# FFN gate/up: chunks 5 and 6 by seven block products

## The chip, the cores and the metric

The kernel runs on one core of a Trainium2 chip. The metric is the device time of one execution in microseconds; the time before is the median of three runs.

## The reference

Three transformer blocks on 256 rows of 1024 features, in float32. Five times in all an FFN is computed, and around them other mixers and embeddings, which the change doesn't touch:

```python
def rms_norm(x, g):
    x32 = x.astype(jnp.float32)
    y = x32 * lax.rsqrt(jnp.mean(x32 * x32, axis=-1, keepdims=True) + EPS)
    return (y * g.astype(jnp.float32)).astype(x.dtype)

def swiglu(h, w_gate, w_up, w_down):
    return (jax.nn.silu(h @ w_gate) * (h @ w_up)) @ w_down
...
        x = x + 0.5 * swiglu(rms_norm(x, g[0]), ffn_w_gate[i, 0], ffn_w_up[i, 0], ffn_w_down[i, 0])
```

The gate and up matrices are 1024x2816, the down matrix 2816x1024.

## The kernel before, in words

**Work.** The 256 rows are two tiles of 128 (tt), the 1024 features eight tiles of 128 (k). The 2816 hidden columns are eleven chunks of 256 (numbered 0 to 10). For a chunk, gate and up columns stand side by side, so that one matmul of 128x512 makes both. The rows are kept transposed and split into a high part (`hth`, rounded to the matmul's type) and a low part (`htl`, the rest); so are weights (`wh`, `wl`). A product of two such numbers is three matmuls (`product`, L273): high by low, high by high, low by high.

**Chunk.** A chunk's gate/up takes 8 k x 2 tiles x 3 = 48 matmuls in two half chunks of 24, called a (k 0 to 3) and b (k 4 to 7) here. They land in PSUM banks 0 and 1 (2 and 3 for chunk 1). The rms scale `rstd` of a row is applied after them. ScalarE does the silu of the gate half (L794), VectorE multiplies it by the up half (L869). The product must be transposed for the down matmuls: VectorE turns 32x32 blocks (L876), ScalarE's queue sends them to DRAM (`move_out`, L799) and back in another order (`move_in`, L803); this way there and back is called the bounce below. Then ScalarE makes the high part (L809), VectorE the low part (L882), and TensorE does the down of that chunk, 24 matmuls into banks 4 to 7, which hold the FFN's result. In the loop the down of chunk c-1 follows the gate/up of chunk c. Chunk 0 and the last are turned by TensorE itself (L666).

**Ring of weights.** Every half chunk and every down has a slot of 128x2048 floats (1 MB). An FFN has 33 slots, in the order a0 b0 a1 b1 d0 a2 b2 d1 a3 b3 d2 and so on. `raw`, `wh` and `wl` have room for three slots each. SP's queue loads a slot when the split of the slot three before it is done (`split_ready`); ScalarE makes its high part when it has landed and TensorE is through with the slot three before (`weights_used`); VectorE makes its low part, the split (L894, outside of the loop L247), and TensorE waits for that.

**Order.** There is no scheduler. Each engine's program is written out by hand: `ffn_load` for SP's queue, `ffn_pe`, `ffn_act`, `ffn_dve`. Within one engine everything goes in that order, and an engine that waits holds up what stands behind. In chunk c of the loop VectorE does: split of d(c-1), low part of product c-1, split of a(c+1), multiply of c, block transpose of c, split of b(c+1). ScalarE does: move_in of c-1, high part of slot d(c-1), of product c-1, of slot a(c+1), silu of c, high part of slot b(c+1), move_out of c. The loops are hardware loops (`Fori`) over chunks 2 to 9.

## Time and profile before

| | |
|---|---|
| median of 3 runs | 1306.96 us (1306.62 to 1307.1) |
| the profiled execution | 1307.18 us, its span 1305.4 us |
| TensorE matmul busy | 1289.2 us, 99% of the span |
| VectorE busy | 846.8 us, 65% |
| ScalarE busy | 654.5 us, 50% |
| GpSimd busy | 83.1 us, 6% |
| HBM read | 243.38 MB |
| mean granted TensorE clock | 0.998 |

The span reaches from the first to the last instruction; the time of an execution is a little longer. Busy times are the union of an engine's instructions. Matmuls overlap in the pipeline, so a busy TensorE need not be one at its peak; the distance from start to start tells what one costs. The page cuts the span into 40 slices: TensorE is busy 90% or more in each but the last, and the DMA engines are 60 to 70% busy in most slices of an FFN.

### The profile page before, as it was taken

What the parts mean: (1) busy time and instruction counts of PE and PEld (TensorE: products, weight loads), DVE (VectorE), ACT (ScalarE), POOL (GpSimd) and SP (SyncE); (2) the same over time, 40 slices, a digit from 0 to 9 for tenths busy, and PEclk for the clock granted to TensorE, in tenths of its full rate; (3) what the DMA queues carried; (4) which work ended last, traced back from release to release, by engine and by line L of the source; (5) the groups of instructions that cost most, each with busy time, mean ns of one, the idle gap of its engine ahead of it and who ended that gap; (6) DMA issues with size and microseconds to landing.
All of it is one profiled execution on the core that took longest, in us unless ns stands there. A gap on an engine that the chain in (4) does not pass through costs nothing.

```text
span 1305.4 us, 17052 instructions
## 1 busy us (share of the span) xinstructions
PE 1289.2 (99%) x6249; PEld 1081.4 (83%) x6249; DVE 846.8 (65%) x929; ACT 654.5 (50%) x769; POOL 83.1 (6%) x195
## 2 busy tenths in 40 slices
PE   9999999999999999999999999999999999999997
PEld 7888889888888887888888877888888987888886
DVE  5665559876555567655556976555567887655554
ACT  6444457445444447544445865444447555544442
POOL 2000004100000002000001300000001300000000
PEclk9999999999999999999999999999999999999999
DMA  9776755446666745666663326666645551676771
GB/s 296 239 231 225 225 194 168 155 136 216 222 225 225 229 173 193 211 225 224 225 225 125 133 97 219 224 225 225 225 177 162 187 175 57 206 226 224 226 227 69
DMA packets 189563, 256.87 MB, mean 197 GB/s; under 512 B 9048, under 2 KB 151022, under 8 KB 189518
## 3 DMA queue, kind: packets, MB, share of 16 engines
q1 hardware_dynamic: 156560, 229.17, 53.3%
q10 hardware_dynamic: 32478, 26.30, 6.4%
q0 software_dynamic: 480, 0.80, 0.4%
q8 instruction: 29, 0.48, 0.1%
q14 instruction: 16, 0.13, 0.0%
HBM read 243.38 MB, written 12.85 MB: 196 GB/s over the span
## 4 chain that ended last, share of the span: by engine, by line
PE 96%; DVE 2%; ACT 1%; issue 0%; POOL 0%; POOLq 0%; DVEq 0%; ACTq 0%
PE ps L275 28%; PE ps L277 28%; PE ps L276 28%; PE ps L372 1%; PE ps L302 1%; PE ps L303 1%; PE ps L304 1%; DVE wl L247 1%; PE ps L1242 1%; PE ps L2972 0%; PE ps L666 0%; PE ps L281 0%; PE ps L2290 0%; PE ps L282 0%; PE ps L285 0%
## 5 line engine op out<-in xcount | busy, mean ns | idle before, releaser
L275 PE MATMUL ps<-wl,hth 128*128 128x512 f32 (+3 forms) x1256 | 490.1, 390 | 1.5 <-DVE htl L2148 0.8
L277 PE MATMUL ps<-wh,htl 128*128 128x512 f32 (+3 forms) x1256 | 485.0, 386 | 0.0
L276 PE MATMUL ps<-wh,hth 128*128 128x512 f32 (+3 forms) x1256 | 484.6, 386 | 0.0
L894 DVE TENSOR_TENSOR wl<-raw,wh 128x2048 fp32r<-128x2048 f32 x120 | 275.1, 2292 | 189.6 <-ACT wh L821 184.4
L821 ACT ACTIVATE wh<-raw 128x2048 fp32r<-128x2048 f32 x120 | 229.5, 1913 | 155.4 <-DMA bounce<-xn 114.8
L275 PEld LDWEIGHTS ps<-wl,hth 128*128 128x128 f32 x1256 | 236.1, 188 | 49.8 <-issue 2.7
L277 PEld LDWEIGHTS ps<-wh,htl 128*128 128x128 f32 x1256 | 236.0, 188 | 47.5
L276 PEld LDWEIGHTS ps<-wh,hth 128*128 128x128 f32 x1256 | 236.2, 188 | 44.8
L247 DVE TENSOR_TENSOR wl<-raw,wh 128x2048 fp32r<-128x2048 f32 (+3 forms) x94 | 207.5, 2216 | 63.1 <-ACT wh L236 62.3
L236 ACT ACTIVATE wh<-raw 128x2048 fp32r<-128x2048 f32 (+3 forms) x94 | 173.5, 1852 | 59.2 <-PE ps L277 43.9
L275 PE MATMUL ps<-wl,prod_h 128*128 128x512 f32 x400 | 156.3, 391 | 0.0
L277 PE MATMUL ps<-wh,prod_l 128*128 128x512 f32 x400 | 155.8, 390 | 0.0
L276 PE MATMUL ps<-wh,prod_h 128*128 128x512 f32 x400 | 155.8, 390 | 0.0
L794 ACT ACTIVATE silu_g<-ps,rstd 128x256 f32<-128x256 f32 x110 | 46.1, 471 | 144.3 <-PE ps L277 144.2
L277 PEld LDWEIGHTS ps<-wh,prod_l 128*128 128x128 f32 x400 | 75.1, 188 | 15.6
L276 PEld LDWEIGHTS ps<-wh,prod_h 128*128 128x128 f32 x400 | 75.1, 188 | 15.4
L275 PEld LDWEIGHTS ps<-wl,prod_h 128*128 128x128 f32 x400 | 75.1, 188 | 15.4
L869 DVE SCALAR_TENSOR_TENSOR prod<-ps,rstd,silu_g 128x256 f32<-128x256 f32 x110 | 48.2, 479 | 57.1 <-ACT silu_g L794 57.1
L809 ACT ACTIVATE prod_h<-xn 128x512 fp32r<-128x512 f32 x45 | 28.5, 632 | 110.9 <-DMA xn<-bounce 110.8
L528 POOL TENSOR_SCALAR mean_sq<-mean_sq 128x1 f32<-128x1 f32 x20 | 9.9, 495 | 825.4 <-ACT xn L515 819.8
L882 DVE TENSOR_TENSOR prod_l<-xn,prod_h 128x512 fp32r<-128x512 f32 x45 | 31.1, 692 | 40.1 <-ACT prod_h L809 40.0
L876 DVE STREAM_TRANSPOSE xn<-prod 128x512 f32<-128x512 f32 x45 | 50.5, 1122 | 1.5
(423 smaller groups left out, 992.6 us busy)
## 6 DMA issues: line engine op xcount, KB each, us to landing
raw<-in_ffn_w_down SPq DMA_DIRECT2D x88, 512.0 KB, 4.0
raw<-in_ffn_w_gate SPq DMA_DIRECT2D x86, 512.0 KB, 4.1
raw<-in_ffn_w_up SPq DMA_DIRECT2D x86, 512.0 KB, 5.1
raw<-in_w_gate_up SPq DMA_DIRECT2D x44, 512.0 KB, 4.8
raw<-in_even_w_in SPq DMA_DIRECT2D x24, 512.0 KB, 4.5
bounce<-xn ACTq DMA_DIRECT2D x45, 256.0 KB, 3.1
xn<-bounce ACTq DMA_DIRECT2D x45, 256.0 KB, 5.1
raw<-in_w_down SPq DMA_DIRECT2D x22, 512.0 KB, 4.2
```

The lines of the kernel that those rows point to most:

```text
L236: nc.scalar.activation(high_of(n)[:, 0:width[n]], raw[:, n % RING, 0:width[n]], ACT.Copy)\
L247: nc.vector.tensor_tensor(low_of(n)[:, 0:width[n]], raw[:, n % RING, 0:width[n]], high_of(n)[:, 0:width[n]].bitcast(f32), ALU.subtract)\
L275: nc.tensor.matmul(o, xh, b, start=first, stop=False)
L276: nc.tensor.matmul(o, xh, a, start=False, stop=False)
L277: return nc.tensor.matmul(o, xl, a, start=False, stop=last)
L794: nc.scalar.activation(silu_g[:, tt, :], ps[:, b + tt, 0:HC], ACT.Silu, scale=rstd[:, tt:tt + 1]).then_inc(silu_ready, 1)
L809: nc.scalar.activation(prod_tiles(prod_h), moved_tiles, ACT.Copy).then_inc(prod_high, 1)
L821: nc.scalar.activation(wh[:, r, :], raw[:, r, :], ACT.Copy).then_inc(high_ready, 1)
L869: m = nc.vector.scalar_tensor_tensor(out=prod[:, tt, :], in0=ps[:, b + tt, HC:2 * HC], scalar=rstd[:, tt:tt + 1], in1=silu_g[:, tt, :], op ...
L876: nc.vector.transpose(prod_blocks.rearrange("p (r g t) -> p g r t", r=4, g=4), prod[:, :, :].rearrange("p t (k n r) -> p (t k) r n", k=2, ...
L882: nc.vector.tensor_tensor(prod_tiles(prod_l), moved_tiles, prod_tiles(prod_h).bitcast(f32), ALU.subtract).then_inc(prod_low, 1)
L894: nc.vector.tensor_tensor(wl[:, r, :], raw[:, r, :], wh[:, r, :].bitcast(f32), ALU.subtract)\
```

## The change

In each of the five FFNs the gate/up of chunks 5 and 6 is done together in Strassen's form (the variant of Winograd with 7 products). The rows by features are a 2x2 matrix of blocks (tile 0 or 1, k 0 to 3 or 4 to 7), the weights another one (k 0 to 3 or 4 to 7, chunk 5 or 6). `near` is chunk 5, `far` chunk 6. In place of eight block products of 12 matmuls there are seven.

- **Rows.** The blocks of rows must carry their rms scale before they are added up, since a sum mixes two tiles. `row_diagonals` makes diagonals of `rstd`, TensorE multiplies them by ones (two small float32 products, `turn_first`) to get the scales as a row, VectorE adds high and low parts of the turned rows (`turned_rows`), multiplies by the row and makes four differences (`mix_rows`); ScalarE and VectorE make their high and low parts. This happens at the start of each FFN.
- **Weights.** The two half chunks of chunk 6 are loaded into the arena on SP's queue behind slot d1 (`load_far`), one of them once more into the ring (b22). VectorE makes four sums (`far_sum`, `near_sums`, `last_sum`); three of them are split apart from the ring, the fourth is written in the ring's place "sum", which is not loaded. The pair's six ring slots become b11, b21, b22, d4, sum, and d5 and d6 come later: the order of slots is a4 b4 d3 b11 b21 b22 d4 sum a7 b7 d6 d5 a8 and so on, still 33.
- **TensorE in the pair** (`pair`): a quarter is 12 matmuls into one bank. Quarters 1 to 6, the down of chunk 4, quarter 7; two quarters accumulate onto the bank of an earlier one. The results are put together by two evictions of ScalarE (`evict`) and five additions of VectorE (`combine`). Chunk 7 uses banks 1 and 2; then come the downs of chunk 6 and of chunk 5.
- **Loops** are written out; the rest of the order is as before. Some arena offsets move.

```diff
+        PAIRS = (5,)
+        ORDER = [("a", 0), ("b", 0), ("a", 1), ("b", 1), ("d", 0)]
+        waiting, c = [1], 2
+        while c < NCH - 1:
+            if c in PAIRS:
+                ORDER += [("b11", c), ("b21", c), ("b22", c), ("d", waiting.pop(0)), ("sum", c)]
+                waiting, c = [c + 1, c], c + 2
+            else:
+                ORDER += [("a", c), ("b", c)] + [("d", w) for w in waiting]
+                waiting, c = [c], c + 1
...
                 for q, g in enumerate(PAIRS):
                     if i == PAIR_LOADS[g]:
+                        sp.wait_ge(weights_used, n + 2)
+                        load_far(sp, len(PAIRS) * f + q, g)
...
+            def turn_first():
+                pe.wait_ge(prod_ready, f * NCH + 1)
+                turn_product(0)
+                pe.wait_ge(mix_diag, f + 1)
+                for tt in range(TT):
+                    m = nc.tensor.matmul(ps[:, 1, tt * P:(tt + 1) * P], ones[:, :], diag[:, tt, :], start=True, stop=True)
+                m.then_inc(mix_row, 1)
...
+            def pair(c):
...
+                pe.wait_ge(sum_low, 3 * q + 1)
+                quarter(3, *of_mix(2), *of_sum(HIGH3, SUM3), True, True).then_inc(sums_used, 1)
+                pe.wait_ge(prod_ready, f * NCH + TURN.index(c - 1) + 1)
+                quarter(0, *near[0], *of_slot("b11", c), True, True).then_inc(weights_used, 1)
+                pe.wait_ge(sum_low, 3 * q + 2)
+                quarter(2, *of_mix(0), *of_sum(HIGH1, SUM1), True, True).then_inc(sums_used, 1)
+                pe.wait_ge(evicted, 2 * q + 1)
+                quarter(0, *near[1], *of_slot("b21", c), False, True).then_inc(weights_used, 1)
+                pe.wait_ge(sum_low, 3 * q + 3)
+                quarter(1, *of_mix(1), *of_sum(HIGH2, SUM2), True, True).then_inc(sums_used, 1)
+                pe.wait_ge(evicted, 2 * q + 2)
+                quarter(2, *of_mix(3), *of_slot("b22", c), False, True).then_inc(weights_used, 1)
+                down(c - 1)
+                pe.wait_ge(combined, 5 * q + 1)
+                quarter(3, *of_mix(4), *of_slot("sum", c), False, True).then_inc(weights_used, 1)
+                pe.wait_ge(combined, 5 * q + 4)
...
             pe.wait_ge(prod_ready, f * NCH + 2)
-            with pe.Fori(2, NCH - 1) as c:
-                chunk(c, False)
+            pe.wait_ge(mix_ready, f + 1)
+            waiting, c = [1], 2
+            while c < NCH - 1:
+                if c in PAIRS:
+                    pair(c)
+                    waiting, c = [c + 1, c], c + 2
+                else:
+                    plain(c)
+                    for w in waiting:
+                        down(w)
+                    pe.wait_ge(prod_ready, f * NCH + TURN.index(c) + 1)
+                    waiting, c = [c], c + 1
...
+            def mix_rows():
+
+                v = rows_turned
+                dve.wait_ge(mix_row, f + 1)
+                dve_link(dve, nc.vector.tensor_tensor(v, v, repeated(bank(1, T), 1, KT), ALU.mult))
+                a11, a12, a21, a22 = (v[:, 4 * half:4 * half + 4, tt * P:(tt + 1) * P] for tt in range(TT) for half in range(2))
+                nc.vector.tensor_tensor(mixed(2), a11, a21, ALU.subtract)
+                dve_link(dve, nc.vector.tensor_tensor(mixed(0), a21, a22, ALU.subtract))
+                dve_link(dve, nc.vector.tensor_tensor(mixed(1), mixed(0), a11, ALU.subtract))
+                nc.vector.tensor_tensor(mixed(3), mixed(1), a12, ALU.add).then_inc(mix_ready, 1)
...
             dve_ahead.through(dve, n + 4)
+            turned_rows()
             low_turned(0, 0, prod_l, prod_h)
             dve_ahead.through(dve, n + 5)
-            multiply(1, 2)
+            mix_rows()
+            multiply(1)
             turn_blocks(1)
+            far_sum(PAIRS[0])
             dve_ahead.through(dve, n + 6)
...
+                if pair_next:
+                    if c + 1 != PAIRS[0]:
+                        far_sum(c + 1)
+                    near_sums(c + 1)
+                    sum_low_of(c + 1, 1, HIGH3, SUM3)
+                    through("b11", c + 1)
...
                 multiply(c)
                 turn_blocks(c)
```

Where VectorE's order moves, first at the start of an FFN (here the first one, from the split of slot d0 on; chunk 1's multiply is the row on `silu_ready`). Before:

```order
L247 TENSOR_TENSOR wl<-raw,wh 128x2048 [waits high_ready,dve_chain]
L887 TENSOR_TENSOR prod_l<-ps,prod_h 128x512 [waits prod_high]
L247 TENSOR_TENSOR wl<-raw,wh 128x2048 [waits high_ready]
L869 SCALAR_TENSOR_TENSOR prod<-ps,rstd,silu_g 128x256 [waits silu_ready] x2
L876 STREAM_TRANSPOSE xn<-prod 128x4x4x32 [waits prod_ready]
```

And now:

```order
L282 TENSOR_TENSOR wl<-raw,wh 128x2048 [waits high_ready,dve_chain]
L1104 TENSOR_TENSOR arena<-hth,htl 128x2048
L1091 TENSOR_TENSOR prod_l<-ps,prod_h 128x512 [waits prod_high,dve_chain]
L282 TENSOR_TENSOR wl<-raw,wh 128x2048 [waits high_ready]
L1110 TENSOR_TENSOR arena<-arena,ps 128x2048 [waits mix_row]
L1112 TENSOR_TENSOR arena<-arena 128x512 [waits dve_chain]
L1113 TENSOR_TENSOR arena<-arena 128x512
L1114 TENSOR_TENSOR arena<-arena 128x512 [waits dve_chain]
L1115 TENSOR_TENSOR arena<-arena 128x512 [waits dve_chain]
L1071 SCALAR_TENSOR_TENSOR prod<-ps,rstd,silu_g 128x256 [waits silu_ready] x2
L1080 STREAM_TRANSPOSE xn<-prod 128x4x4x32 [waits prod_ready]
L1138 TENSOR_TENSOR arena<-arena 128x2048 [waits sum_loaded1,sum_loaded0]
```

Two items of 2048 and four of 512 now stand ahead of chunk 1's multiply, and one of 2048 behind its transpose. The second place is chunk 4, on VectorE, from the low part of product 3 on. Before (a turn of the loop, whose first row here is that low part):

```order
L882 TENSOR_TENSOR prod_l<-xn,prod_h 128x512 [waits prod_high]
L893 REGISTER_ALU
L894 TENSOR_TENSOR wl<-raw,wh 128x2048 [waits high_ready]
L868 ISA
L869 SCALAR_TENSOR_TENSOR prod<-ps,rstd,silu_g 128x256 [waits silu_ready]
L868 REGISTER_ALU
L869 SCALAR_TENSOR_TENSOR prod<-ps,rstd,silu_g 128x256 [waits silu_ready]
```

And now:

```order
L1087 TENSOR_TENSOR prod_l<-xn,prod_h 128x512 [waits prod_high]
L1146 TENSOR_TENSOR arena<-arena,raw 128x2048 [waits mix_low,sum_ready,raw_loaded2]
L1147 TENSOR_TENSOR arena<-arena,raw 128x2048
L1162 TENSOR_TENSOR arena_r<-arena,arena_r 128x2048 [waits sum_ready,sum_high]
L282 TENSOR_TENSOR wl<-raw,wh 128x2048 [waits high_ready]
L1071 SCALAR_TENSOR_TENSOR prod<-ps,rstd,silu_g 128x256 [waits silu_ready] x2
L1080 STREAM_TRANSPOSE xn<-prod 128x4x4x32 [waits blocks_out,prod_ready]
L1162 TENSOR_TENSOR arena_r<-arena,arena_r 128x2048 [waits sum_high]
L282 TENSOR_TENSOR wl<-raw,wh 128x2048 [waits high_ready]
L1153 TENSOR_TENSOR raw<-arena,raw 128x2048 [waits raw_loaded0,sum_ready,split_ready]
L1162 TENSOR_TENSOR arena_r<-arena,arena_r 128x2048 [waits last_sum_ready,sum_high]
L282 TENSOR_TENSOR wl<-raw,wh 128x2048 [waits high_ready]
```

Where one split stood between that low part and chunk 4's multiply, there are two sums, a low part of a sum and a split. The third place is ScalarE in the pair, around the bounce of product 4; L943 is now move_out, L949 move_in, L959 the high part of the product, L980 and L983 are the evictions:

```order
L271 ACTIVATE wh<-raw 128x2048 [waits weights_used,raw_loaded0]
L943 DMA bounce<-xn 128x512 [waits blocks_ready]
L271 ACTIVATE wh<-raw 128x2048 [waits weights_used,raw_loaded1]
L949 DMA xn<-bounce 128x4x128 [waits prod_low,blocks_out]
L980 ACTIVATE xn<-ps,rstd 128x512 [waits weights_used]
L959 ACTIVATE prod_h<-xn 128x512 [waits weights_used,blocks_moved]
L271 ACTIVATE wh<-raw 128x2048 [waits weights_used,raw_loaded2]
L983 ACTIVATE xn<-ps 128x512 [waits sums_used]
```

Both evictions are new; each stands behind a part of the bounce.

## Rows read from the trace of the kernel before

**Rows 1.** The page: busy time by engine, and the chain's shares by engine

```profile
PE 1289.2 (99%) x6249; PEld 1081.4 (83%) x6249; DVE 846.8 (65%) x929; ACT 654.5 (50%) x769; POOL 83.1 (6%) x195
...
PE 96%; DVE 2%; ACT 1%; issue 0%; POOL 0%; POOLq 0%; DVEq 0%; ACTq 0%
```

**Rows 2.** Waits of PE, whole run, longest: waited for; us, times, longest

```profile
PE ps L2972 <- POOL ident L2901: 1.6, 1, 1.6
...
PE ps L687 <- ACT wh L228: 0.7, 1, 0.7
```

**Rows 3.** Timeline of PE, first FFN, sixty matmuls apart: start, duration, line

```profile
60.53 0.39 PE L275 MATMUL ps<-wl,hth 128*128 128x512 f32 x1
...
74.13 0.39 PE L275 MATMUL ps<-wl,hth 128*128 128x512 f32 x1
```

**Rows 4.** Groups by line (busy us, mean ns), and a piece of the chain

```profile
L894 DVE TENSOR_TENSOR wl<-raw,wh 128x2048 fp32r<-128x2048 f32 x120 | 275.1, 2292 | 189.6 <-ACT wh L821 184.4
L821 ACT ACTIVATE wh<-raw 128x2048 fp32r<-128x2048 f32 x120 | 229.5, 1913 | 155.4 <-DMA bounce<-xn 114.8 <-PE ps L277 40.5
...
L876 DVE STREAM_TRANSPOSE xn<-prod 128x512 f32<-128x512 f32 x45 | 50.5, 1122 | 1.5
L869 DVE SCALAR_TENSOR_TENSOR prod<-ps,rstd,silu_g 128x256 f32<-128x256 f32 x110 | 48.2, 479 | 57.1 <-ACT silu_g L794 57.1
L794 ACT ACTIVATE silu_g<-ps,rstd 128x256 f32<-128x256 f32 x110 | 46.1, 471 | 144.3 <-PE ps L277 144.2
L882 DVE TENSOR_TENSOR prod_l<-xn,prod_h 128x512 fp32r<-128x512 f32 x45 | 31.1, 692 | 40.1 <-ACT prod_h L809 40.0
...
L809 ACT ACTIVATE prod_h<-xn 128x512 fp32r<-128x512 f32 x45 | 28.5, 632 | 110.9 <-DMA xn<-bounce 110.8
...
199.51 0.45 PE ps L574 x4
```

**Rows 5.** Timeline, start of the second FFN: split of d0, transposes, split of a2

```profile
315.98 2.29 DVE L247 TENSOR_TENSOR wl<-raw,wh 128x2048 fp32r<-128x2048 f32 x1 [0.61 <-ACT wh L236]
...
318.49 0.60 PE L666 MATMUL ps<-ident,prod 128*128 128x128 f32 x4
...
321.56 2.29 DVE L247 TENSOR_TENSOR wl<-raw,wh 128x2048 fp32r<-128x2048 f32 x1 [1.11 <-ACT wh L236]
```

**Rows 6.** The same two, transposes and split of d0, first and last FFN

```profile
26.72 0.60 PE L666 MATMUL ps<-ident,prod 128*128 128x128 f32 x4
27.39 2.29 DVE L247 TENSOR_TENSOR wl<-raw,wh 128x2048 fp32r<-128x2048 f32 x1 [0.48 <-ACT wh L236]
...
1133.16 2.29 DVE L247 TENSOR_TENSOR wl<-raw,wh 128x2048 fp32r<-128x2048 f32 x1 [1.29 <-ACT wh L236]
...
1134.39 0.60 PE L666 MATMUL ps<-ident,prod 128*128 128x128 f32 x4
```

**Rows 7.** Timeline, second FFN: bounce of product 4, high part, silu and multiply of 5

```profile
376.15 0.34 ACTq L799 DMA_DIRECT2D bounce<-xn  x1
379.63 0.37 ACTq L803 DMA_DIRECT2D xn<-bounce  x1
...
384.90 0.63 ACT L809 ACTIVATE prod_h<-xn 128x512 fp32r<-128x512 f32 x1 [2.80 <-DMA xn<-bounce]
...
389.90 0.84 ACT L794 ACTIVATE silu_g<-ps,rstd 128x256 f32<-128x256 f32 x2 [2.56 <-PE ps L277]
...
390.41 0.88 DVE L869 SCALAR_TENSOR_TENSOR prod<-ps,rstd,silu_g 128x256 f32<-128x256 f32 x2 [0.75 <-ACT silu_g L794]
```

**Rows 8.** Landing times of the bounce's two transfers (L799, then L803)

```profile
DMA to landing us min/median/max: 2.0/3.1/4.5
...
DMA to landing us min/median/max: 2.7/5.1/5.9
```

**Rows 9.** Windows: us, PE busy (matmuls), granted PE clock, DMA share, GB/s

```profile
750.00:765.00 15.00, 13.05 (x71) 1.00 0.19 72
...
495.00:511.00 16.00, 16.00 (x73) 1.00 0.98 324
```

More of the change, by code:

```diff
@@ L858, in ffn_act @@
+            silu(c)
+            if late is not None:
+                high(late)
             act_ahead.through(act, n + FFN_SLOTS)
@@ L897, in ffn_dve, with through @@
+            def through(kind, c):
+                dve_ahead.through(dve, n + PLACE[kind, c])
             if after_ple(s):
@@ L931, in ffn_dve @@
+                c += 1
             multiply(NCH - 1)
+            if late is not None:
+                low(late)
             dve_ahead.through(dve, n + FFN_SLOTS)
```

468 lines of the change are left out of this document (348 added, 120 removed).

## The prediction, made before the change was run

> **What bounds the kernel now.** I read the page's busy table and its chain first: TensorE is busy 99% of the span and makes up 96% of the chain that ended last [rows 1]. Then I asked who TensorE waits for: the longest wait of the whole execution is 1.6 us, at the start, and in the first FFN it waits for nobody inside the chunks [rows 2]. So removed matmuls shorten the program one for one, and a microsecond that TensorE waits lengthens it by one, unless something later had to wait anyway. The price of a 128x512 matmul is not its duration, 386 to 391 ns, since matmuls overlap: sixty of them start between 60.53 and 74.13 us, so one costs **0.2267 us** [rows 3]. A gate/up half chunk (24) is 5.44 us, a down piece 5.44, a chunk 16.32.
>
> Then the covering engines. Per chunk VectorE does three splits, a product's low half, two multiplies and a block transpose: 3 x 2.29 + 0.69 + 2 x 0.48 + 1.12 = 9.6 us of 16.3; ScalarE three high halves, one of the product and two silus [rows 4]. VectorE has 6.7 us per chunk to spare, on average. But every engine works its queue in order, and the weight ring is three slots deep, so what matters is whether each item is in time.
>
> **What goes.** Two chunks' gate/up are 96 matmuls; seven quarters of 12 are 84. That is 12 x 0.2267 = 2.72 us per FFN, **13.6 us** over five. TensorE gains two ones-times-diagonal products for the row of scales, four records as in an earlier use of the same form, 0.45 us [rows 4]: 2.3 us over five. If TensorE never waited, the change would be worth 11.3 us. The reordered downs (chunk 6's before chunk 5's) cost nothing in themselves: same matmuls, other order.
>
> **What VectorE gets**, per FFN: four sums of weights (2048 wide), three low halves of sums, the turned rows added, their scaling and the low halves of the mixed rows make ten items of 2.29; ten of 512 wide at 0.69. The ring keeps its 33 slots, so no split goes. That is 30 us, 150 us in all: the 847 of the busy table [rows 1] become about 1000 of 1300. On average it fits. ScalarE gets three high halves of sums, one and a quarter for the rows and two evictions, some 9.5 us. None of these shapes with a PSUM operand is in the trace at 2048; the bounds are the 2.29 of the SBUF form, and that plus the few hundredths by which 128x512 forms differ. What matters is four places.
>
> *1. Start of an FFN.* Let T be the start of the first product's transposes. TensorE then does 0.35 + 0.45 + 5.44 (half chunk) + 5.44 (first down) and some 0.15 for the starts after narrow products: it wants chunk 2 at T+11.85. There it now waits for the mixed rows and chunk 1's product. VectorE's queue from the end of the first down slot's split: turned rows 2.29, low half of product 0 0.69, split 2.29, scaling 2.29, four differences 4 x 0.69, multiply 0.88: 11.2 us without a gap. In the last FFN that split ends at T+1.06 [rows 6]: 12.25, a wait of 0.4; the third and fourth read within 0.05 us of it. In the second it ends at T-0.2 and the next split begins at T+3.1 [rows 5]: ready at 11.3, no wait. In the first it ends at T+3.0 [rows 6], and the diagonals (0.6) come ahead of its small steps: 14.8, a wait of 2.9. Together **4 us**. If queued items start 0.08 before the end of the one ahead of them it is 2.5; if each of the three steps that wait for the one before costs 0.3 more, 8.
>
> *2. First down of the loop.* The multiply of chunk 1, and with it its bounce, leaves about 4 us later than now; then ScalarE does the rows' high halves (2.5 us) ahead of the second bounce transfer, and VectorE the far sum, a split and the low halves (2.29 + 0.69). The chain bounce (8.5 us), high, low ends at about T+23.2, wanted at T+22.85: 0.3 us each, **1.5 us**. The far sum also waits for 2 MB that SP issues behind the down slot's load; at the 324 GB/s that the full DMA engines show [rows 9] the 3 MB take 10 us from T+1 and are in time for T+13. The other loads on SP's queue behind them (chunk 3's) then land by T+17 and are wanted at T+21: free.
>
> *3. Ahead of the pair.* In a chunk that starts at C the product's high half starts now at C+6.1 (C = silu's start less 11.1) after a bounce of 8.75 [rows 7], and VectorE has its low half at C+7.5. Because of place 2 the bounce is still about 1 us late in chunk 4: C+8.4 (7.5 if it has caught up, 11 if not at all). Only then come the two near sums, the first sum's low half, a split, 4 x 2.29 + 0.88, and that multiply is what TensorE waits for before the first quarter, though the first quarter doesn't read it. It ends at C+18.2; TensorE is there at C+16.3. I take **1.7 us** each, 8.5 in all (0.8 to 4.4 each). Before the change the multiply ended at C+12.5. Behind it wait the block transpose, the bounce of product 4 and all the pair's low halves.
>
> *4. In and behind the pair.* Counting from that multiply's end M, the quarters find their operands: second sum's low half M+3.3 (wanted 5.5), b21 5.6 (8.2), third sum 10.2 (10.9), evictions 6.4 and 12.9 (8.2 and 13.7), product 4 and its slot 15 (16.4), combinations 20 (24.5). Chunk 7's first slot is split at M+24.5 and wanted at 24.5. Its second: ScalarE's second bounce transfer of product 6 stands ahead of that high half, so it is split at 30.2, wanted at 30.0. Product 5 goes out at 32.2, 8.7 us of bounce, high and low: 42.2, wanted at 41.1. Sum **1.3 us** each, 6.5 in all (0 to 3).
>
> The bounce is the soft number: its transfers land in 2.0 to 4.5 and 2.7 to 5.9 us [rows 8]. With both at their upper ends and 0.3 us between them it takes 10.7 us, 2.2 more than I take; in place 2 alone that is 11 us over the five FFNs, and the sum would be 1327 in place of 1316. I keep the ordinary value, since the far loads should be through when the first bounce starts. The Trainium skill (DMA: Bandwidth & Descriptors, Issuing engines are not separate DMA queues) says that the DMAs of all issuing engines run on the same 16 engines and interleave, which speaks for the upper ends; the landing times, whose longest is twice the shortest for one and the same transfer, agree.
>
> **The sum**, against the profiled execution's own 1307.18 us (span 1305.4 and 1.8 around it; the median of the runs is 1306.96): - 13.6 + 2.3 + 4.0 + 1.5 + 8.5 + 6.5 = +9.2, so **1316.4 us**.
>
> **Rivals.**
> *A, the cover holds.* If bounces come in at 6.4 us instead of 8.7, as their landing times allow, places 2, 3 and 4 vanish and only the start's 4 us stay: -13.6 + 2.3 + 4.0 = -7.3, 1299.9 us; with half of the waits left 1304. For it: the trace has such bounces, and VectorE and ScalarE are idle 35% and 50%. Against it: the second FFN repeats 8.75 chunk after chunk. It decides from 2.3 us of bounce per product. 0.21 for all results over 0.2% faster.
> *B, a draw.* The waits eat the gain just: 11.3 us of waits where I have 20.5. 0.12.
> *C, queues pile up.* ScalarE's queue holds a transfer, two evictions and three sums in the pair; if each of the four places costs 1 us more per FFN, it is 20 us more: 1336. It decides where product 3 is still 3.6 us late at the pair. 0.17.
> *D, the clock.* TensorE has never waited over 1.6 us, and with 2 us of 15 idle its granted clock stays 1.00 [rows 9], the 2.4 GHz level; at 1.2 GHz every microsecond of matmuls becomes two, so one chunk spent so in each FFN costs 16 x 5 = 80 us. The Trainium skill (TensorE: Matmul & The Clock Gate, HAM oscillation) says that idle gaps of TensorE send its clock back to half. The new gaps are 0.3 to 2.9 us; no row here shows a fall. 0.02.
> That the change does not do what it says can be excluded: TensorE's order has seven groups of twelve in the pair, and the eleven downs of an FFN are all there.
>
> **How the numbers follow.** Slower by over 0.2% (2.6 us, about what a measurement here can tell from no change) is my forecast at 0.48, C and D: 0.67. Same 0.12, faster 0.21. The forecast's own range, places at their bounds, is 1309 to 1325. For eight in ten I go down to 1302, between a draw and the full cover, and up to 1330, into C.
>
> **What would show it.** TensorE's busy time falls by 11 us and idle time of about 20 appears where there is none: at chunk 2 waiting for the product or the mixed rows (large in the first FFN, small in others), at the first quarter waiting for the multiply (1 to 3 us, five times), at chunk 7's second half and at product 5's down, waiting for low halves. VectorE near 1000 us busy. DMA reads 5 MB more. It is wrong if the first quarter starts without a wait, or if the multiply of chunk 1 comes before TensorE has finished its first down in every FFN.

## The result, and the profile after

The changed kernel takes **1350.8 us** (median of 4 runs, 1348.5 to 1356.4), the kernel before 1306.8 on the same chip: a ratio of 1.034, interval 1.031 to 1.038. That is 44 us slower, where 9.4 were predicted; the direction was right, the range (to 1330) was not. The profiled execution is the longest of the four, 1356.42 us, 49.2 above its counterpart before, and all times below that are read from its trace belong to those 49.2. One of the four runs of quarter_early below took 1602.2 us at a mean granted clock of 0.753; it is left out of that version's time.

The page of the changed kernel, busy time and the chain's shares (as [rows 1]):

```profile
PE 1299.6 (96%) x6209; PEld 1079.9 (80%) x6209; DVE 980.0 (72%) x1039; ACT 697.3 (51%) x804; POOL 81.8 (6%) x195
...
PE 54%; DVE 20%; DMA 14%; ACT 6%; issue 4%; SPq 1%; ACTq 0%; POOL 0%; DVEq 0%; POOLq 0%
```

TensorE has 40 instructions fewer and is nevertheless busy 10 us longer, and the chain, which before was TensorE for 96%, goes through VectorE and DMA for a third. Whom TensorE waits for (as [rows 2], where the longest wait was 1.6 us), the same kernel:

```profile
PE ps L310 <- DVE prod_l L1087: 14.4, 5, 3.9
PE ps L310 <- DVE prod L1071: 14.1, 6, 3.0
PE ps L310 <- DVE htl L1091: 6.9, 4, 2.0
PE ps L3309 <- POOL ident L3238: 1.6, 1, 1.6
```

L1087 writes a product's low half, L1071 is the multiply, L1091 the low half of the last product, turned by TensorE. The timeline of the same kernel gives the places (start, duration, what is multiplied, in brackets the wait and its releaser):

```profile
40.69 0.79 PE L310 MATMUL ps<-wl,hth 128*128 128x512 f32 x1 [2.15 <-DVE prod L1071]
93.64 0.50 PE L310 MATMUL ps<-arena_r 128*128 128x512 f32 x1 [2.15 <-DVE prod L1071]
138.94 0.50 PE L310 MATMUL ps<-wl,prod_h 128*128 128x512 f32 x1 [3.88 <-DVE prod_l L1087]
197.69 0.50 PE L310 MATMUL ps<-wl,hth 128*128 128x512 f32 x1 [1.95 <-DVE htl L1091]
...
437.90 0.50 PE L310 MATMUL ps<-wl,prod_h 128*128 128x512 f32 x1 [3.01 <-DVE prod_l L1087]
```

In order: chunk 2 of the first FFN, the pair's first quarter, product 5's down, the last chunk's down at an FFN's end, and product 5's down in the second FFN. The first quarter waits in all five FFNs (2.15, 1.66, 2.25, 2.93, 2.96 us: 12.0), product 5's down too (3.88, 3.01, 3.51, 2.21, 1.77: 14.4), an FFN's end in four of five, chunk 2 in the first alone.

The same trace gives the ledger of the FFNs. From the transposes of product 0 to those of the last product an FFN took 155.5 us before, in each of the five; now 165.9, 158.9, 163.0, 165.1 and 161.8, together 37.0 more. Counting how far consecutive matmuls start apart, and taking 0.2267 us [rows 3] off each: 31.7 us stand at the listed waits, **12.7 us in 72 matmuls that start 0.33 to 0.43 us apart**, nearly all close behind waits, and 3.7 are smaller remainders. 31.7 + 12.7 + 3.7 less the 11.3 of matmuls saved is 36.8, against the 37.0 read. The other 12.2 us lie outside these stretches, 6.9 of them the waits on L1091.

54 of these 72 matmuls, 10.7 us, are the clock; the other 18 are for the most part second matmuls behind a wait, which start 0.34 us after the first at the full clock too. Behind the wait of 3.88 us at product 5's down:

```profile
139.28 0.39 PE L311 MATMUL ps<-wh,prod_h 128*128 128x512 f32 x1
139.51 0.56 PE L312 MATMUL ps<-wh,prod_l 128*128 128x512 f32 x1
...
140.29 0.63 PE L311 MATMUL ps<-wh,prod_h 128*128 128x512 f32 x1
140.72 0.63 PE L312 MATMUL ps<-wh,prod_l 128*128 128x512 f32 x1
```

and windows of that trace (us, PE busy and its matmuls, granted clock, DMA share, GB/s):

```profile
137.00:141.00 4.00, 2.06 (x6) 0.82 0.20 73
141.00:145.00 4.00, 4.00 (x14) 0.75 0.57 145
...
438.00:442.00 4.00, 4.00 (x18) 1.00 0.27 86
```

The second and third matmul behind the wait start 0.23 us apart, those from 139.86 us on 0.43, about twice that: the granted clock has gone to its lower level of 1.2 GHz for some 3 us. It does so behind six of the eleven waits of over 1.5 us inside the FFNs (3.88, 3.51, 2.96, 2.93, 2.21 and one of 2.15 us) and not behind the others (3.01, 2.25, the other 2.15, 1.77 and 1.66). A seventh fall, of seven such matmuls, stands outside, behind one of the four waits at an FFN's end (1.95 us, at 719.44 us). The mean granted clock of the four runs is 0.987 to 0.992, 0.998 before.

Two causes are to be seen at once in the traces. At an FFN's end VectorE before the change does one split, then the last product's low half; first the kernel before, then the changed one:

```profile
182.40 2.29 DVE L247 TENSOR_TENSOR wl<-raw,wh 128x2048 fp32r<-128x2048 f32 x1 [1.29 <-ACT wh L236]
184.61 0.69 DVE L887 TENSOR_TENSOR htl<-ps,hth 128x512 fp32r<-128x512 f32 x1
```

```profile
192.54 4.49 DVE L282 TENSOR_TENSOR wl<-raw,wh 128x2048 fp32r<-128x2048 f32 x2 [1.29 <-ACT wh L271]
196.95 0.68 DVE L1091 TENSOR_TENSOR htl<-ps,hth 128x512 fp32r<-128x512 f32 x1
```

Two splits stand there now, where one did: with the loop written out, the split of slot d10, which stood ahead of the last chunk's silu and multiply, stands behind them. And product 5's way through HBM, in the second FFN of the changed kernel, beside what SP issues:

```profile
422.38 0.38 SPq L207 DMA_DIRECT2D raw<-in_ffn_w_gate  x1
...
426.99 0.37 SPq L207 DMA_DIRECT2D raw<-in_ffn_w_gate  x1
...
429.19 0.81 SPq L207 DMA_DIRECT2D raw<-in_ffn_w_down  x2
```

```profile
424.22 0.34 ACTq L943 DMA_DIRECT2D bounce<-xn  x1
429.32 0.37 ACTq L949 DMA_DIRECT2D xn<-bounce  x1
...
436.49 0.63 ACT L959 ACTIVATE prod_h<-xn 128x512 fp32r<-128x512 f32 x1 [5.92 <-DMA xn<-bounce]
```

From issue to the high half it takes 12.3 us; [rows 7] had 8.75. In the five FFNs it is 12.0, 12.3, 11.7, 12.4 and 11.9. SP issues 3 MB, slots a8, b8 and d7, around it, six transfers from 2 us before the way out to 5.4 us behind it. Product 4, with none issued while it is under way, takes 6.1 to 8.1 us; product 7, with four, 8.9 to 11.5.

### The profile page after: what moved, and what is told of

Its sections match the earlier page's. It is cut to its first block, busy times and chain, and to the rows that moved or that the text cites. A ratio compares the mean times of both kernels' runs of the same rounds, so it can differ in the third digit from the quotient of the medians.

```text
span 1354.6 us, 15698 instructions
## 1 busy us (share of the span) xinstructions
PE 1299.6 (96%) x6209; PEld 1079.9 (80%) x6209; DVE 980.0 (72%) x1039; ACT 697.3 (51%) x804; POOL 81.8 (6%) x195
## 4 chain that ended last, share of the span: by engine, by line
PE 54%; DVE 20%; DMA 14%; ACT 6%; issue 4%; SPq 1%; ACTq 0%; POOL 0%; DVEq 0%; POOLq 0%
PE ps L310 15%; PE ps L312 15%; PE ps L311 15%; DVE wl L282 8%; DMA xn<-bounce 6%; DMA bounce<-xn 5%; ACT wh L271 3%; DVE arena_r L1162 2%; DMA arena<-in_ffn_w_up 1%; DVE prod L1071 1%; DVE xn L1080 1%; DMA raw<-in_ffn_w_up 1%; PE ps L407 1%; DVE arena L1146 1%; DVE arena L1147 1%
## 5 line engine op out<-in xcount | busy, mean ns | idle before, releaser
L282 DVE TENSOR_TENSOR wl<-raw,wh 128x2048 fp32r<-128x2048 f32 (+2 forms) x214 | 480.7, 2255 | 163.5 <-ACT wh L271 161.5
L271 ACT ACTIVATE wh<-raw 128x2048 fp32r<-128x2048 f32 (+2 forms) x214 | 401.8, 1885 | 203.8 <-PE ps L312 96.5
L310 PE MATMUL ps<-wl,hth 128*128 128x512 f32 (+2 forms) x1136 | 446.0, 393 | 11.9 <-DVE htl L1091 6.9
L312 PE MATMUL ps<-wh,htl 128*128 128x512 f32 (+2 forms) x1136 | 439.4, 387 | 0.0
L311 PE MATMUL ps<-wh,hth 128*128 128x512 f32 (+2 forms) x1136 | 439.3, 387 | 0.0
L310 PEld LDWEIGHTS ps<-wl,hth 128*128 128x128 f32 x1136 | 214.5, 189 | 60.2 <-DVE htl L1091 8.8
L312 PEld LDWEIGHTS ps<-wh,htl 128*128 128x128 f32 x1136 | 214.3, 189 | 43.5
L311 PEld LDWEIGHTS ps<-wh,hth 128*128 128x128 f32 x1136 | 214.6, 189 | 40.3
L310 PE MATMUL ps<-wl,prod_h 128*128 128x512 f32 x360 | 144.2, 401 | 14.4 <-DVE prod_l L1087 14.4
L1071 DVE SCALAR_TENSOR_TENSOR prod<-ps,rstd,silu_g 128x256 f32<-128x256 f32 x95 | 41.7, 478 | 58.1 <-ACT silu_g L932 58.1
L959 ACT ACTIVATE prod_h<-xn 128x512 fp32r<-128x512 f32 x40 | 25.2, 629 | 69.4 <-DMA xn<-bounce 69.2
L427 ACT ACTIVATE hth<-ps,cols 128x256 fp32r<-128x256 f32 x69 | 27.2, 474 | 52.5 <-PE ps L407 52.4
L1087 DVE TENSOR_TENSOR prod_l<-xn,prod_h 128x512 fp32r<-128x512 f32 x40 | 27.5, 688 | 34.9 <-ACT prod_h L959 34.8
L440 DVE SCALAR_TENSOR_TENSOR htl<-ps,cols,hth 128x256 fp32r<-128x256 f32 x69 | 28.8, 478 | 17.8 <-ACT hth L427 17.6
```

Of the source, the lines that this page charges most:

```text
L271: nc.scalar.activation(high_of(n)[:, 0:width[n]], raw[:, n % RING, 0:width[n]], ACT.Copy)\
L282: nc.vector.tensor_tensor(low_of(n)[:, 0:width[n]], raw[:, n % RING, 0:width[n]], high_of(n)[:, 0:width[n]].bitcast(f32), ALU.subtract)\
L310: nc.tensor.matmul(o, xh, b, start=first, stop=False, skip_group_check=onto)
L311: nc.tensor.matmul(o, xh, a, start=False, stop=False, skip_group_check=onto)
L312: return nc.tensor.matmul(o, xl, a, start=False, stop=last, skip_group_check=onto)
L427: m = nc.scalar.activation(dst[:, k, :], ps[:, banks[b], o:o + T], ACT.Copy, scale=g)
```

## The experiments

Each run has the kernel before beside it on its chip (1306.8 to 1307.2); ratios are to it. Edits are to the changed kernel unless another is named.

### First round: what costs nothing, what the end costs, and the clock

**no_pair** leaves the pair and the rows' mixings out and keeps the written-out loops.

```diff
-        PAIRS = (5,)
+        PAIRS = ()
...
-            row_diagonals()
...
-            turned_rows()
...
-            mix_rows()
...
-            far_sum(PAIRS[0])
...
-            mix_low_parts()
```

> The changed kernel with an empty list of pairs and none of the rows' mixing: same plain chunks as before, but loops written out and the changed queue order at an FFN's end. If the cost lies in the pair's waits: 1307 plus what the end order costs, five times 1.5 to 2 us, so 1314 to 1318, with a wait of TensorE for the last product's low half in each FFN. If written-out code costs by itself (fetching of instructions, other issue times): over 1325, with losses spread over all chunks.

Measured: 1315.3 us, ratio 1.007 (1.005 to 1.009). Its FFNs take 155.53 us again, and the one new wait is the end's:

```profile
PE ps L310 <- DVE htl L1085: 6.9, 4, 2.0
```

So the written-out loop, with its other order at the end, costs 8.4 us by itself, 6.9 of them in four waits.

**tail** puts that order back.

```diff
                 c += 1
+            dve_ahead.through(dve, n + FFN_SLOTS - 1)
             multiply(NCH - 1)
```

(on ScalarE the same, ahead of the last silu)

> The changed kernel with the split of slot d10 back ahead of the last multiply, on ScalarE and VectorE. If the wait at an FFN's end (6.9 us in four FFNs) comes from that order: that wait is gone and the time falls from 1350.8 by 7 to 10 us, to about 1342. If the wait comes from the lateness that the pair leaves behind: it stays, and the time with it.

Measured: 1341.7 us, 1.026 (1.025 to 1.028): 9.1 less. The wait on the last low half is gone, the others stay, 13.5 us at the multiplies and 12.8 at product 5's down.

**quarter_early** drops TensorE's wait for chunk 4's multiply ahead of the first quarter, which doesn't read it.

```diff
-                    pe.wait_ge(prod_ready, f * NCH + TURN.index(c) + 1)
+                    if c + 1 not in PAIRS:
+                        pe.wait_ge(prod_ready, f * NCH + TURN.index(c) + 1)
```

> The changed kernel without TensorE's wait for chunk 4's multiply ahead of the first quarter, which doesn't read it (the second quarter still waits). If each wait is paid by itself: the five waits of 1.7 to 3.0 us go, 1350.8 less 12 to 15 us, about 1338. If the chain through VectorE's queue and product 5's bounce sets the end of the pair: TensorE arrives earlier at product 5's down and waits there longer by as much, and the time stays within 4 us of 1350.8.

Measured: 1355.7 us, 1.037 (1.034 to 1.041), 4.9 us above the changed kernel, whose runs spread over 8: nothing won. The waits moved:

```profile
PE ps L310 <- DVE prod_l L1088: 18.0, 5, 4.5
...
PE ps L310 <- DVE arena_r L1163: 3.9, 6, 1.2
PE ps L310 <- DVE wl L282: 3.1, 8, 0.8
PE ps L310 <- DVE prod L1072: 2.2, 1, 2.2
```

A wait taken away in front of a later one that is bound by something else (here product 5's way) is only handed on.

**filled** keeps TensorE at work with unread matmuls (128x512, 0.2267 us each) ahead of the long waits.

```diff
+            if s == 0:
+                fill(0, 9)
...
+                        if w in PAIRS:
+                            pe.wait_ge(combined, 5 * (f + 1))
+                            fill(3, 8)
...
+                    if c + 1 in PAIRS:
+                        fill(3, 7)
```

> The changed kernel with extra matmuls that nobody reads, in front of the long waits: 9 at the first FFN's start, 7 ahead of the first quarter, 8 ahead of product 5's down, 128x512 of one pass each. They take 0.2267 us each and fit inside the waits. If the granted clock falls because TensorE stands idle, the mean clock returns from 0.987-0.992 to about 0.998 and the time falls by 10 to 17 us, to about 1337, though TensorE does more. If the clock is no cost: 1351 or a little more.

Measured: 1342.8 us, 1.028 (1.026 to 1.030), 8.0 less, mean clock 0.995 to 0.997. More matmuls and a shorter time: the fall of the clock is real and follows TensorE's idleness, since nothing else was taken away. The gain is below the 10 to 17 us expected: the clock still falls three times, where it fell seven times (behind 1.96 us left at product 5's down and behind 1.96 and 1.95 us at two FFNs' ends, which were not filled), and long waits are only filled, not gone. The clock is the smaller part of the 44 us.

### Second round: product 5's way, and VectorE's queue

**held** lets SP's loads for slot b8, and all behind it, wait for product 5's return.

```diff
+                    if (kind, c) == ("b", PAIRS[0] + 3):
+                        sp.wait_ge(blocks_moved, 16 * (f * (NCH - 2) + TURN.index(PAIRS[0])))
```

> The change, with SP's loads for slot b8 and all behind them held until product 5's columns have come back from HBM. Theory 1 (the bounce of product 5 takes 12.1 us instead of 8.7 because SP's loads for slots a8, b8 and d7 are under way beside it): its mean over the five FFNs falls to 8.5 to 10 us, the five waits at product 5's down fall from 14.4 us in sum to 2 to 6, and with less of the clock's fall the time comes 8 to 14 us below the change, 1337 to 1343. Rival (the bounce is slow for reasons of its own, such as the queue it is issued on or its number in the FFN): it stays at 12, the waits stay at 14, and the time stays within 3 us of 1350.8, or is above it where the held loads come too late for chunk 8.

Measured: **1329.0 us**, 1.018 (1.015 to 1.020): 21.8 less, by one wait more. Product 5 in the second FFN, and SP's queue (slot a8 goes out, b8 is held):

```profile
419.68 0.34 ACTq L945 DMA_DIRECT2D bounce<-xn  x1
423.97 0.37 ACTq L951 DMA_DIRECT2D xn<-bounce  x1
...
426.59 0.63 ACT L961 ACTIVATE prod_h<-xn 128x512 fp32r<-128x512 f32 x1
```

```profile
417.83 0.38 SPq L207 DMA_DIRECT2D raw<-in_ffn_w_gate  x1
...
426.59 0.37 SPq L207 DMA_DIRECT2D raw<-in_ffn_w_gate  x1
```

6.9 us in place of 12.3; the five are 6.7, 6.9, 6.9, 7.3 and 7.7, below even the 8.75 of [rows 7]. No wait is left at product 5's down, and the same ledger gives 15.3 us of waits and 6.4 of slow matmuls, where 31.7 and 12.7 were. Product 7 now takes 10.6 to 11.2 us, beside the loads let go, and nobody waits for it. My theory had the cause; I had put the gain at 8 to 14, since I left out most of what the clock and the time behind each wait give back.

**no_sums** cuts VectorE's four sums of weights to 16 of 2048 columns, so most of the sums is left out.

> The change with VectorE's four sums of weights for each half cut to their first 16 columns: most of the sums of weights is left out. Theory (VectorE's queue ahead of chunk 4's multiply sets when the first quarter may start, and chunk 5's and product 5's work behind it): the waits at the first quarter (12.0 us in the five FFNs) fall to under 2 us in sum, those at product 5's down fall too, but only by as much of them as is not the bounce, to 8 to 14 us; the time falls by 12 to 20 us, clock included, to 1331 to 1339. Rival (ScalarE's silu or the transposes of product 4 set it): the first quarter's waits stay above 8 us in sum and the time falls by under 5 us.

Measured: 1333.7 us (1328.5 to 1341.6), 1.019 (1.016 to 1.022). The waits at the first quarter fall from 12.0 to 6.1 us, where under 2 were expected, and those at product 5's down from 14.4 to 11.6. VectorE's queue holds the first quarter, as thought, but not alone: 0.8 to 1.2 us stay in four of the FFNs and 2.0 in the last. There VectorE itself waits, for ScalarE's silu, here in the second FFN:

```profile
390.54 0.88 DVE L1071 SCALAR_TENSOR_TENSOR prod<-ps,rstd,silu_g 128x256 f32<-128x256 f32 x2 [1.27 <-ACT silu_g L932]
```

On ScalarE that silu stands behind the high halves of two sums, 3.7 us, so the rival named above holds at least a part of what is left. The same 1.27 us stand there in all five FFNs.

**late_5** moves chunk 5's down behind chunk 8's gate and up.

```diff
-                ORDER += [("a", c), ("b", c)] + [("d", w) for w in waiting]
-                waiting, c = [c], c + 1
+                now = waiting[:1] if c - 2 in PAIRS else waiting
+                ORDER += [("a", c), ("b", c)] + [("d", w) for w in now]
+                waiting, c = waiting[len(now):] + [c], c + 1
```

> The change with the down product of chunk 5 moved one slot back, behind chunk 8's gate and up, so that a whole gate/up pass of 27 us more lies between product 5's multiply and its down. Theory: its five waits (14.4 us) vanish with the clock's fall behind them (of the 37 us that the FFNs gained, some 17 to 20), and the time is 1330 to 1336; the first quarter's waits stay at 12 us. Rival (the wait only moves to the next down, as it did from the first quarter to product 5 in the run without that wait): 8 us or more of waits stand at the down of chunk 7 or 8, and the time is above 1342.

Measured: 1333.0 us, 1.020 (1.018 to 1.023), 17.8 less, as expected; no new wait at a down, but 1.4 and 0.3 us ahead of chunk 8 in two FFNs. It is the other cure for the same wait, and product 5's wait with its clock is thus worth about 18 to 22 us.

**all_moves** joins tail, late_5 and chunk 4's turn, silu and multiply ahead of the last sums' work.

> The change with three moves together: the last chunk's silu and multiply behind the turn of the chunk ahead of it, as before the change; chunk 4's turn, silu and multiply ahead of the last sums of weights on VectorE and ScalarE; chunk 5's down behind chunk 8's gate and up. Theory (all of the 44 us are waits of TensorE and the clock's fall behind them): the end of the FFN gives 9, product 5's down 15 to 20, and the first quarter up to 12 and its share of the clock, so 1300 to 1315. Rival (the sums moved behind the multiply come too late for the pair's high quarters, or chunk 7's): new waits stand inside the pair, and the time is 1318 to 1335.

Measured: 1325.5 us, 1.013 (1.010 to 1.016). The rival came true:

```profile
PE ps L311 <- DVE wl L283: 10.0, 12, 1.7
PE ps L311 <- DVE arena_r L1168: 8.0, 5, 2.8
```

The multiply came in time, at the price of the operands of the quarter itself (L1168 is the low half of a sum) and of splits (L283).

### Third round: the three cures together

**held_tail** is held with tail.

> The change with SP's loads held as in the run of that name, and the last chunk's silu and multiply behind the turn of the chunk ahead of it as before the change. Theory (three causes side by side: the slow bounce, the order at an FFN's end, the wait at the first quarter): the two gains add, 21.8 and 9.1 us, so 1320 (1317 to 1323), with the first quarter's waits of 12 to 13 us left. Rival (they share a resource, so that one uncovers the other): waits on the last low parts of the FFN return and it stays above 1325.

Measured: 1324.4 us, 1.013 (1.011 to 1.015). Of tail's 9.1 us 4.6 came: its waits are gone, but the multiplies' grew from 13.1 to 15.0, and the clock of the profiled execution was lower, 0.993 after 0.995.

**held_tail_early** adds to held_tail chunk 4's silu, multiply and turn one split sooner, ahead of the split of the pair's first block.

```diff
                     sum_low_of(c + 1, 1, HIGH3, SUM3)
+                    multiply(c)
+                    turn_blocks(c)
                     through("b11", c + 1)
```

> The same with chunk 4's silu, multiply and turn one split ahead of where they stand (ahead of the split of the pair's first block, behind the low part of the first sum). Theory (VectorE's queue sets the wait at the first quarter): its multiply starts 2.3 us sooner, the first quarter's waits fall from 11 us in the five FFNs to 0 to 3, and the time is 1304 to 1311, about that of the kernel before. Rival (the split that now comes later is the one that the pair's next quarter waits for, or product 4's move is held up): a wait of 1 us or more stands at the second quarter or ahead of chunk 7, and the time is 1314 or more.

Measured: 1317.8 us, 1.009 (1.007 to 1.011). The time is the rival's (1314 or more), though no wait reaches 1 us where the rival has it:

```profile
PE ps L310 <- DVE wl L282: 4.2, 12, 0.7
PE ps L310 <- DVE prod L1076: 3.0, 3, 2.0
PE ps L310 <- DVE arena_r L1167: 2.7, 5, 0.6
```

The waits on the multiply went from 15.0 to 3.0 us (1.95 at the start), and small ones came at the quarters.

**held_tail_nowait** is held_tail without TensorE's wait ahead of the first quarter.

> Loads held, the end's order as before, and TensorE's wait for chunk 4's multiply ahead of the first quarter dropped. With the loads not held, this moved the wait to product 5's down. Theory (there it was product 5's slow bounce that took it up): with a bounce of 7 us no wait of over 1 us stands at product 5's down, the first quarter waits at most for its sum's low parts, and the time is 1303 to 1310. Rival (what came later on ScalarE and VectorE stays later): 5 us or more of waits stand at product 5's down or at the quarters, and the time is 1313 or more.

Measured: 1316.9 us, 1.007 (1.005 to 1.008). With product 5's way short, the edit that won nothing in quarter_early wins 7.5 us, and nothing stands at product 5's down; but 4.4 us of waits for sums' low halves and 3.5 for splits keep it off the 1303 to 1310.

**held_tail_early_fill** adds the unread matmuls to held_tail_early.

> The run with loads held, the end's order and the early multiply, with unread matmuls ahead of the start's, the first quarter's and product 5's down's waits as in the run named filled: some 9 at the start, 7 and 8 in each FFN. Where no wait of 2 us is left, as the theory has it, there is no clock to win, and the added matmuls (75 of some 0.12 us, 9 us of which most no longer fit into waits) cost 3 to 10 us against the run without them. Rival (the clock still falls at waits of 0.5 to 2 us): it is faster than that run by 2 us or more, with a mean granted clock nearer 0.998.

Measured: 1323.2 us, 1.012 (1.010 to 1.014), 5.5 more. The trace has 84 of these matmuls, 0.227 us each and not the 0.12 expected, 19 us in all, of which the time shows 5.5. Where next to no long wait is left, filling only costs.

### Fourth round: where the matmuls saved had gone

held_tail_early's long waits are gone, its clock is 0.997 to 0.999, and still it is 10.7 us above the kernel before. The next runs ask whether small waits, or the block products themselves, hold that back. All move work on VectorE alone, but for one wait of TensorE.

**all_five** is held_tail_early with the first near sum ahead of product 3's low half, and the rows' four differences behind chunk 1's multiply, with TensorE's wait for the mixed rows gone. (all_six, which also drops the wait of quarter_early, gave 1313.4, the same.)

> The run with loads held, the end's order and the early multiply, and two moves more on VectorE: the first of the two sums with the pair's first block goes ahead of the low part of product 3 (which VectorE waits 0.6 to 1 us for), and at an FFN's start chunk 1's multiply and turn go behind the rows' scaling alone, the four mixings behind them, with TensorE's wait for the mixings gone. Theory (the 19 us by which that run's FFNs are above their matmuls are waits of 0.3 to 2 us that VectorE's queue sets, and one fall of the clock at the start): 2.2 us sooner on VectorE takes away nearly all of the waits inside the pair, and the start's goes with its fall of the clock, so 11 to 15 us of the 19, and the time is 1302 to 1308: the seven block products are then worth at most what they cost. Rival (something else than VectorE's queue holds the quarters, such as the landing of the blocks themselves or ScalarE's high parts): waits of 0.5 us or more stay at the pair's quarters, the time is 1312 or more.

Measured: 1312.8 us, 1.004 (1.003 to 1.005), 4.9 less, above the 1302 to 1308 of the theory. The start's wait moved one split on, and the clock fell there:

```profile
46.23 0.50 PE L310 MATMUL ps<-wl,hth 128*128 128x512 f32 x1 [2.22 <-DVE wl L282]
...
47.44 0.63 PE L311 MATMUL ps<-wh,hth 128*128 128x512 f32 x1
```

**far_later** is all_five with the sum of the far blocks moved from ahead of the split of slot b2 to behind product 1's low half.

> The run all_five with the sum of the far blocks moved on VectorE from ahead of the sixth split of an FFN to behind product 1's low parts. In all_five that split started at 43.90 us behind the sum's 2.2 us and was waited for by 2.2 us in the first FFN and 1.9 in the fifth, each with eight matmuls at 0.43 us behind it. Theory: both waits and both falls of the clock go (about 7 us), and the time is 1305 to 1308, level with the kernel before. Rival (the sum is now late for the pair, or the split waits for its load): a wait of 0.5 us or more stands elsewhere and the time is 1311 or more.

Measured: 1320.4 us, 1.010 (1.008 to 1.011), 7.5 more: a miss. The two waits at the split are gone, but the sum now stands ahead of chunk 2's splits, and hands its 2.2 us from product to product: 8.8 us of waits at the downs of chunks 1 to 3, in 12 places.

**near_sooner** is far_later with both near sums in VectorE's idle time around the split of product 3's down weights.

> The run far_later with both sums that take the pair's first block put into VectorE's idle 4 us around the split ahead of product 3's low part. Theory (the waits of 0.3 to 0.6 us at the pair's third and fifth quarters are VectorE's queue still): they go, some 5 us more, so 1300 to 1304 and below the kernel before. Rival (the first block has not landed there, so that VectorE stands and holds up the split of product 3's down weights): waits of 1 us or more at that down, and the time is above that of far_later.

Measured: 1311.7 us, 1.003 (1.002 to 1.005). No wait is left in the pair; the downs' waits are:

```profile
PE ps L310 <- DVE prod_l L1091: 8.3, 10, 1.8
```

**far_idle** is near_sooner with the sum of the far blocks moved once more, into VectorE's idle time ahead of product 2's down weights.

```diff
+                    if c == 2:
+                        far_sum(PAIRS[0])
                     if c + 2 in PAIRS:
                         near_sum_1(c + 2)
                     through("d", c)
```

> The run near_sooner with the sum of the far blocks put into VectorE's idle time ahead of the split of product 2's down weights, where it delays neither a product's low part nor a gate's split. Theory (in near_sooner the downs of chunks 1 to 3 wait 8.3 us in ten places, because the sum stands ahead of chunk 2's split and hands its 2.2 us on from product to product): these waits fall to 2 to 5 us in sum, and the time is 1305 to 1309, within 0.2% of the kernel before. Rival (the products' bounces set these downs by themselves): the waits stay above 7 us and the time at 1311 to 1313.

Measured: **1307.1 us** (median of 11 runs, 1305.5 to 1309.0), ratio 1.0000 (0.999 to 1.001): level with the kernel before, 43.6 us below the change with the same work. Its waits and its chain:

```profile
PE ps L310 <- DVE prod_l L1091: 4.7, 6, 1.7
```

```profile
PE 78%; DVE 9%; DMA 7%; ACT 4%; issue 2%; ACTq 0%; POOL 0%; DVEq 0%; POOLq 0%
```

Its FFNs take 156.4, 153.6, 155.6, 154.1 and 155.7 us. In the second TensorE waits nowhere for 0.2 us, and it is 1.9 us shorter than before, of the 2.3 that the prediction gives for matmuls saved less the diagonals. So where nothing waits, the block products bring nearly what their count says; the waits that are left, and what lies outside the FFNs, spend it. No version was faster than the kernel before by more than a measurement tells.

## Why the prediction was wrong, step by step

**What goes** (13.6 us less 2.3) was right: the second FFN of far_idle shows 1.9 of 2.3 us, and the kernel with all its waits hides it. **What VectorE gets** was right, 980 us of busy time against about 1000.

**Place 1, start of an FFN** was priced at 4 us, 2.9 in the first FFN and 0.4 in three others. It was 2.15 in the first and none in the rest (0.5 and 0.6 us stand one split later in the last two). **Place 2, first down of the loop** (1.5) was nearly nothing. **Place 3, ahead of the pair** (8.5) was 12.0, inside its bounds of 4 to 22, at the place and on the releaser named. The chain was right as well: the low half of product 3 ended 8.3 to 9.6 us behind the chunk's start (8.4 taken), the multiply 18.1 to 19.4 (18.2), and TensorE was there at 16.3. The 1.7 us taken for each is a slip, since 18.2 less 16.3 is 1.9. VectorE works with next to no gap up to the multiply, here in the first FFN of the changed kernel:

```profile
83.71 2.28 DVE L1146 TENSOR_TENSOR arena<-arena,raw 128x2048 f32<-128x2048 f32 x1
85.91 2.29 DVE L1147 TENSOR_TENSOR arena<-arena,raw 128x2048 f32<-128x2048 f32 x1
88.30 2.29 DVE L1162 TENSOR_TENSOR arena_r<-arena,arena_r 128x2048 fp32r<-128x2048 f32 x1
90.51 2.28 DVE L282 TENSOR_TENSOR wl<-raw,wh 128x2048 fp32r<-128x2048 f32 x1
92.71 0.87 DVE L1071 SCALAR_TENSOR_TENSOR prod<-ps,rstd,silu_g 128x256 f32<-128x256 f32 x2
```

no_sums and held_tail_early show that queue as the cause, with ScalarE's silu close behind it.

**Place 4, in and behind the pair** is the step that failed most. It had product 5's down wait 1.1 us in each FFN and chunk 7's second half 0.2; the down waited 2.9 on average, 14.4 in all. The chain of times was right but for one term: "8.7 us of bounce" was 12.0 on average, 3.3 more. Product 5 went out 30.8 to 32.8 us behind the multiply's end M (32.2 forecast), and its low half was there at 44.4 to 46.5 (42.2). TensorE came at 41.3 (41.1) in three FFNs. In the other two it came at 44.1 and 42.9, late by the fall of the clock behind the first quarter's wait, which is why their waits were only 2.2 and 1.8. "The bounce is the soft number" named it, and gave 10.7 us as its upper end; but it looked at the places at an FFN's start and took the pair's bounce at its ordinary value, without asking what SP issues just then. Behind the pair VectorE does the splits of two down slots back to back (4.49 us from 424.68 on, in the second FFN), and at the end of each SP issues 1 MB more (426.99 and 429.19), just ahead of the bounce's way back at 429.32. held shows it: the loads kept back, the bounce is 7.1 us and the time 21.8 less. The ordinary value itself was read in one FFN: products 1 to 8 of the kernel before take 8.7 to 9.2 us in the first two FFNs, but 6.4 to 8.1 in the third. The Trainium skill (DMA: Bandwidth & Descriptors, Issuing engines are not separate DMA queues) says that transfers of all issuing engines interleave on the same engines; the two bounces, 12.0 and 7.1 us for one and the same product, agree, and the rule was quoted in the prediction without its consequence for this place.

**"The reordered downs cost nothing in themselves"**, and with it the silent assumption that the loops written out keep the order elsewhere, missed the end of an FFN: 6.9 us of waits, 8.4 to 9.1 us of time (no_pair, tail). The sum has no term for it, and the description of the change says of the order "as before", which is not so there. The diff had it: on ScalarE and VectorE the last chunk's silu and multiply now stand ahead of slot d10's high half and split, and the order of VectorE's instructions at that place shows one split more.

**Rival D, the clock**, had a chance of 0.02 and the sentence that no row shows a fall. It came in part: not at half speed for whole chunks (80 us), but for 6 to 13 matmuls behind seven of the waits, 10.7 us in the FFNs of the profiled execution. A reader of the waits predicted (2.9 us in the first FFN) should have seen that the trace before has no wait above 1.6 us, so that it could not speak about them. The sum had each wait at its bare length; with the clock and the slow start behind it, 14.4 us at product 5's down were worth 18 (late_5) to 22 us (held).

In short: 20.5 us of waits forecast, and in the profiled execution about 37 listed, plus about 13 of slow matmuls. **What would show it** failed in its first sentence: busy time did not fall by 11 us, it rose by 10, since slow matmuls count as busy, and so does the end of a matmul that a wait follows. Its waits at chunk 2, the first quarter and product 5's down came, and so did VectorE's 980 us and 5.2 MB more read.

**Rival C** (queues pile up, 1336) was nearer than the forecast, for another reason: its four places did not each cost 1 us more, one cost 1.8 more in each FFN.

## What to carry to other kernels

When a kernel is bound by one engine without gaps, price a change by where it puts gaps, and a gap at more than its length, since the clock may fall behind it. For every latency-bound transfer on the new critical chain, list what the other queues issue in the same microseconds: holding back loads that aren't urgent was one line and worth 22 us here. And where a loop is written out anew, compare the order of each engine's instructions at its ends as well as in the part that was changed.

## What the runs showed of the hardware

In the changed kernel the clock fell to its lower level behind seven waits of 1.95 to 3.88 us, for 6 to 13 matmuls at 0.43 us each, and in all_five behind two of 2.22 and 1.92 us; behind one of 3.01 us it did not, nor behind two others of 2.15 and 2.25. The length of a wait alone does not decide it. The kernel before, whose waits are all below 1.7 us, has no such matmul in any of its five FFNs. The Trainium skill (TensorE: Matmul & The Clock Gate, HAM oscillation) describes such falls for a kernel that waits for DMA at every step; here a single wait did it, the engine being busy without a gap ahead of it and behind it.

One and the same bounce of 256 KB out and 256 KB back took 6.7 to 7.7 us with loads held and 11.7 to 12.4 with 3 MB of loads beside it; the way back alone, in the second FFN, 2.6 against 7.2 us, with the DMA engines 34% busy against 86%. Repeated runs of kernels with many waits spread over 2 to 13 us (near_sooner's over 1), those of the kernel before over 1. My reading, which no run tests: where a wait ends by a race between transfers, and the clock may fall behind it, a few tenths decide several microseconds.

Left open: what decides whether the clock falls behind a wait, and whether a last 2 us could be won at product 1's down in the first FFN of far_idle (1.7 us), which wasn't tried.
